# RWKV row pairs of a fused fp32 kernel: the 16x16 diagonal blocks of the chunk inverse move from TensorE products to elementwise VectorE work with transfers through DRAM, some row tensors move into PSUM banks, and the sums over 64 channels become two fp32r passes

## The reference, cut to what is touched

```python
k_mod = k.astype(f32) * (1.0 + (a - 1.0) * k_a)
kk = heads(k * k_k)
kk = kk / jnp.maximum(jnp.sqrt(jnp.sum(kk * kk, axis=-1, keepdims=True)), 1e-12)
def step(state, inp):
    r_t, w_t, k_t, v_t, aa_t, bb_t = inp
    sa = jnp.einsum('bhvk,bhk->bhv', state, aa_t)
    state = state * w_t[:, :, None, :] + sa[..., None] * bb_t[:, :, None, :] + v_t[..., None] * k_t[:, :, None, :]
    return state, jnp.einsum('bhvk,bhk->bhv', state, r_t)
...
var = jnp.mean(jnp.square(y - mean), axis=-1, keepdims=True)
y = ((y - mean) * lax.rsqrt(var + GN_EPS)).reshape(b, s, c) * lnx_w + lnx_b
bonus = (jnp.sum(r_h * k_h * r_k, axis=-1, keepdims=True) * v_h).reshape(b, s, c)
```

## Time and profile before

| | |
|---|---|
| runs, median of 3 | 2084.86 us (2081.75 to 2087.8) |
| profiled execution | 2081.08 us, of which the span is 2079.3 us |
| busy share of the span | PE 98%, PEld 81%, POOL 57%, DVE 55%, ACT 26% |
| mean granted TensorE clock | 0.995 |

### The profile page before, as it was taken

How to read it: one execution, slowest core, us unless ns; L and a number is a source line. 1 busy time by engine, 2 the same in 40 slices (tenths; PEclk the granted TensorE clock), 3 DMA queues, 4 the chain that set the end, 5 groups by cost and what they waited for, 6 DMA issues and landing times.

```text
span 2079.3 us, 39898 instructions
## 1 busy us (share of the span) xinstructions
PE 2031.4 (98%) x16195; PEld 1678.5 (81%) x16195; DVE 1139.5 (55%) x1533; ACT 536.0 (26%) x1139; POOL 1178.7 (57%) x1175
## 2 busy tenths in 40 slices
PE   8999999999999999999999999999999999999998
PEld 6888888877877787788877888888886888888886
DVE  6878624466667654202068677666773655555312
ACT  2100002233434212313143133333223023333101
...
GB/s 136 102 92 102 101 101 46 92 176 121 127 163 112 148 82 64 98 62 61 124 56 93 15 65 66 46 48 46 65 65 124 133 101 81 101 99 90 89 112 56
DMA packets 181243, 190.28 MB, mean 92 GB/s; under 512 B 8526, under 2 KB 162269, under 8 KB 180829
## 3 DMA queue, kind: packets, MB, share of 16 engines
q1 hardware_dynamic: 172288, 181.81, 27.6%
...
## 4 chain that ended last, share of the span: by engine, by line
PE 61%; DVE 3%; issue 1%; POOL 1%; DVEq 1%; POOLq 1%; ACT 0%; ACTq 0%
PE bank L915 8%; PE bank L916 8%; PE bank L917 8%; PE bank L1592 7%; PE bank L1553 3%; PE bank L1405 3%; PE bank L1421 2%; PE bank L1423 2%; PE bank L1422 2%; PE bank L1690 2%; PE bank L1327 1%; PE bank L1328 1%; PE bank L1329 1%; PE bank L1080 1%; PE bank L1294 1%
## 5 line engine op out<-in xcount | busy, mean ns | idle before, releaser
L740 POOL TENSOR_SCALAR whi<-raws 128x1024 fp32r<-128x1024 f32 (+5 forms) x312 | 321.0, 1029 | 284.9 <-PE bank L1082 166.8
L746 POOL TENSOR_TENSOR wlo<-raws,whi 128x512 fp32r<-128x512 f32 (+5 forms) x312 | 400.8, 1285 | 0.0
L745 POOL TENSOR_TENSOR wlo<-raws,whi 128x512 fp32r<-128x512 f32 (+5 forms) x312 | 373.4, 1197 | 46.0 <-issue 3.0
L915 PE MATMUL bank<-hbuf,whi 128*128 128x512 f32 (+2 forms) x840 | 329.4, 392 | 1.8 <-POOL wlo L746 1.8
L917 PE MATMUL bank<-hbuf,wlo 128*128 128x512 f32 (+2 forms) x840 | 327.8, 390 | 0.0
L916 PE MATMUL bank<-hbuf,whi 128*128 128x512 f32 (+2 forms) x776 | 303.0, 390 | 0.0
L649 POOL TENSOR_TENSOR spare<-ones 1x1 f32<-1x1 f32 x92 | 21.4, 233 | 298.5 <-PE bank L917 208.2
L915 PEld LDWEIGHTS bank<-hbuf,whi 128*128 128x128 f32 (+2 forms) x840 | 157.1, 187 | 37.0 <-POOL wlo L746 3.1
L917 PEld LDWEIGHTS bank<-hbuf,wlo 128*128 128x128 f32 (+2 forms) x840 | 157.1, 187 | 34.1
L916 PEld LDWEIGHTS bank<-hbuf,whi 128*128 128x128 f32 (+2 forms) x776 | 145.2, 187 | 31.1
L672 POOL TENSOR_SCALAR lg2L<-lg 128x128 fp32r<-128x128 f32 x8 | 2.4, 298 | 221.7 <-DMA lg<-in_g 221.7
...
## 6 DMA issues: line engine op xcount, KB each, us to landing
...
raws<-in_w_in SPq DMA_DIRECT2D x41, 512.0 KB, 3.9
...
```

The source lines that it names most:

```text
L740: G.tensor_scalar(h_, r_, 1.0, 1.0, ALU.mult, ALU.mult)
L745: G.tensor_tensor(first[0], first[1], f32(first[2]), ALU.subtract)
L746: G.tensor_tensor(last[0], last[1], f32(last[2]), ALU.subtract).then_inc(raw_split, 1)
L915: M.matmul(dst, wh, acts[k][0], start=(first and k == 0), stop=False)
```

## The change

It has four parts.

1. **Block inverse.** `LEVELS` keeps 5 products in 4 levels, those that join blocks of 16 to 32 and 64. The 16x16 blocks are inverted by VectorE on 64 partitions (`inverted_blocks`), one block per partition and pair of columns. For that `diagonal_blocks` packs the blocks out of the product D, ACT writes them to DRAM and reads them back with a block on a partition (`blocks_gathered`), and the result goes the same way back (`blocks_kept`, `blocks_spread`), a chunk later each, and is spread by VectorE (`spread_blocks`) into `V` and `W`. The product D now stands in `gates`, after 6 matmuls.
2. **Row in PSUM banks.** Squares, key directions, lengths, decays and deviations of a row use banks 3, 4, 5 and 7 in place of tiles of SBUF; the factor of the decays moves into ACT's scale; `finished` moves from the wide part into the next chain.
3. **Sums.** For rows 2 to 7 each head sum takes two fp32r matmuls: ACT makes the upper part by a cast, VectorE the lower part by a subtraction, and each sum waits for `sum.lo`.
4. **Slots.** The 12 products left in `prepare` stand in slots 1, 2, 6, 7, 9, 10, 12, 14, 16, 17, 19 and 21; slots 0, 3 to 5, 8, 11, 13, 15, 18, 20, 22 and 23 are empty.

The core of the diff:

```diff
-    (("DA", "D", "N2"), ("D", "DA", "A2")),
-    (("N2", "A2", "A4"), ("A2", "U", "U")),
-    (("A4", "U", "V"),),
-    (("A4", "V", "V"),),
-    (("A4", "V", "V"),),
-    (("V", "I", "W"), ("E16", "V", "Z")),
+    (("E16", "V", "Z"),),
     (("W", "Z", "V"), ("Z", "W", "W")),
     (("E32", "V", "Z"),),
     (("W", "Z", "last"),),
...
+BLOCKS_KEPT_AT = (3, 2, 2, 2, 2, 2, 3)
...
-LEVEL_BANK = ((1, 6),) * 7 + ((7,), (6,))
+LEVEL_BANK = ((1,), (1, 6), (7,), (6,))
+D_AFTER = 6
...
+            def head_sums(dst, q, which):
+
+                hi, lo = sum_split(q, which)
+                pe.wait_ge(sem("sum.lo"), sum_number(q, which))
+                M.matmul(dst[:, :], same64[:, :], hi, start=True, stop=False)
+                return M.matmul(dst[:, :], same64[:, :], lo, start=False, stop=True)
+
...
-                rkv(0, 2)
+                rkv(0, 6)
                 if q >= 2:
                     variances(q - 2)
-                rkv(2, 8)
+                rkv(6, 8)
                 if q >= 2:
                     pe.wait_ge(sem("inv.dve"), q * TAKEN_ALL)
-                    bonus_sums(q - 1)
                 else:
                     pe.wait_ge(sem("gt.taken"), 2)
-                rkv(8, 16)
+                rkv(8, 10)
+                if q >= 2:
...
 
                 pe.wait_ge(evac[0], fill("rkv", 0) + q + 1)
-                for n in range(3 * DT):
+                for n in range(D_AFTER):
                     gate_part(q, n)
-                pe.wait_ge(sem("rk.bonus"), q)
-                pe.wait_ge(sem("rk.y"), q)
+                gram(q, "D")
+                for n in range(D_AFTER, 3 * DT):
+                    gate_part(q, n)
+                pe.wait_ge(sem("rk.sig"), q + 1)
                 for n in range(3 * DT, 6 * DT):
                     gate_part(q, n)
 
...
+            def upper_sum(q, which, x):
+
+                A.copy(sum_split(q, which)[0], x).then_inc(sem("sum.hi"), 1)
...
+                    A.activation(tile(sq, 0), Kr[:, :], ACT.Square, scale=pcol[q % 3][:, 5:6]).then_inc(sem("rk.sq"), 1)
+                else:
+                    act.wait_ge(sem("gn.v"), q - 1)
+                    A.activation(bank[7][:, :], Kr[:, :], ACT.Square, scale=pcol[q % 3][:, 5:6])
+                    act.drain()
+                    upper_sum(q, "key", bank[7][:, :])
...
+            def blocks_gathered(q):
+
+                act.wait_ge(sem("blk.d"), q + 1)
+                act.dma_start(blocks_in[q % 2].rearrange("(c p j) -> p c j", c=CHUNKS, p=P),
+                              diagonal.rearrange("p (c j) -> p c j", c=CHUNKS)).then_inc(sem("blk.kept"), 16)
+                act.wait_ge(sem("blk.kept"), 16 * (q + 1))
+                act.dma_start(blk, blocks_in[q % 2].rearrange("(n x) -> n x", n=64)).then_inc(sem("blk.in"), 16)
+
+            def blocks_kept(q):
+
+                act.wait_ge(sem("blk.x"), q + 1)
+                act.dma_start(blocks_out[q % 2].rearrange("(w n x) -> n w x", w=2, n=64),
+                              hf[0:64, 0:2 * BLK * BLK].rearrange("n (w x) -> n w x", w=2)).then_inc(sem("blk.out"), 16)
+
+            def blocks_spread(q):
+
+                act.wait_ge(sem("blk.out"), 16 * (q + 1))
+                act.dma_start(hf[:, S + P:S + 3 * P].rearrange("p (x j) -> p x j", j=BLK),
+                              blocks_out[q % 2].rearrange("(x p j) -> p x j", p=P, j=BLK)).then_inc(sem("blk.back"), 16)
+
             def take_gates(q):
 
                 take_gate(q, 0)
+                if q >= 2:
+                    blocks_gathered(q)
                 take_gate(q, 1)
 
 
...
                     A.copy(sa[:, :], bank[5][:, cs]).then_inc(sem("sq.se"), 1)
+                    if p + 1 < PAIRS and c == BLOCKS_KEPT_AT[p]:
+                        blocks_kept(p + 1)
+                    if p + 1 < PAIRS and c == BLOCKS_KEPT_AT[p] + 1:
+                        blocks_spread(p + 1)
                     if c + 1 < CHUNKS:
...
+            def key_directions(q):
+
+                lengths = bank[3]
+                dve.wait_ge(sem("rk.nr"), q + 1)
...
+                dve.drain()
+                V.scalar_tensor_tensor(lengths[:, :], Kr[:, :], pcol[q % 3][:, 5:6], lengths[:, :], ALU.mult, ALU.mult)
...
+                V.scalar_tensor_tensor(aT[par][:, :], direction[:, :], -1.0, lwd[:, :], ALU.mult, ALU.mult)
+                dve.drain()
+                V.tensor_tensor(direction[:, :], direction[:, :], cc[:, :], ALU.mult)
+                dve.drain()
+                V.tensor_tensor(bT[:, :], direction[:, :], aa[:, :], ALU.mult).then_inc(sem("rk.ab"), 1)
+                dve.drain()
+                V.tensor_scalar(change[:, :], aa[:, :], pc[:, 6:7], pc[:, 10:11], ALU.mult, ALU.add)
...
+
+            def lower_sum(q, which, x):
+
+                hi, lo = sum_split(q, which)
+                dve.wait_ge(sem("sum.hi"), sum_number(q, which))
+                V.tensor_tensor(lo, x, f32(hi), ALU.subtract).then_inc(sem("sum.lo"), 1)
...
                     columns_of(q)
+                    lower_sum(q, "variance", gn_sq[:, :])
                     log_decays(q)
+                    lower_sum(q, "bonus", Rr[:, :])
                     take_key(q)
                 take_bonus(q - 1)
+                if 2 <= q < PAIRS:
+                    lower_sum(q, "key", bank[7][:, :])
                 if more:
                     take_product(q, 0, Rr)
-                if q >= 2:
+                if q == PAIRS:
+                    deviations(q - 2)
                     finished(q - 2)
-                if more:
+                if q == 1:
                     take_product(q, 2, vT[q % 2])
...
-                gram("D")
-                taken(inv_D, 1, "up16")
+                if q >= 2:
+                    inverted_blocks(q)
                 gram("A")
...
-                take_level(0)
-                take_turned(vtok, 7, "rk.tv")
                 if q == 0:
                     key_directions(1)
-                take_level(1)
+                if q < 2:
+                    inverted_blocks(q)
+                else:
+                    finished(q - 2)
                 gram("qb")
                 taken(Gqb[q % 2], 0, "up0")
-                take_level(2)
+                take_turned(vtok, 7, "rk.tv")
+                take_turned(kN, 0, "rk.tk")
                 take_turned(bN[q % 2], 7, "rk.tb")
-                take_level(3)
-                take_turned(kN, 0, "rk.tk")
-                take_level(4)
-                gram("qk")
-                taken(Gqk, 7, "up0")
                 if q == 0:
+                    gram("qk")
+                    taken(Gqk, 7, "up0")
                     decayed_keys(1)
...
+                dve.wait_ge(sem("blk.back"), 16 * (q + 1))
+                spread_blocks(V, inv_D, blk_v).then_inc(sem("inv.v"), 1)
+                spread_blocks(V, tile(hf, 0), blk_w).then_inc(sem("inv.w"), 1)
+                if q:
+                    gram("qk")
+                    taken(Gqk, 7, "up0")
+                else:
+                    dve.drain()
+                for k in range(len(LEVELS)):
                     take_level(k)
                 dve.drain()
+                if q == 0:
+                    diagonal_blocks(1)
+
+            def diagonal_blocks(q):
+
+                dve.wait_ge(sem("rk.block"), q + 1)
+                masked(inv_D, bank[1], "up16")
+                dve.drain()
+                V.tensor_reduce(diagonal.rearrange("p (c j) -> p c j", c=CHUNKS),
+                                inv_D[:, :].rearrange("p (c b j) -> p c j b", c=CHUNKS, j=BLK), AX.X, ALU.add)\
...
+            def inverted_blocks(q):
+
+                dve.wait_ge(sem("blk.in"), 16 * (q + 1))
+                V.memset(blk[:, 0:BLK * BLK:BLK + 1], 1.0)
...
+                for m in (4, 8):
+                    n, cube = BLK // (2 * m), [64, m, m, m]
+
...
+                    def times(lefts, rights):
+                        for b in range(n):
+                            terms = blk_terms[:, b * m ** 3:(b + 1) * m ** 3]
+                            V.tensor_tensor(terms.rearrange("n (i j k) -> n i j k", i=m, j=m),
+                                            lefts[b].unsqueeze(2).to_broadcast(cube),
+                                            rights[b].rearrange("n k j -> n j k").unsqueeze(1).to_broadcast(cube),
+                                            ALU.mult)
+                        dve.drain()
...
+                    half = blk_half[:, 0:n * m * m]
+                    V.tensor_reduce(half, blk_terms[:, 0:n * m ** 3].rearrange("n (x k) -> n x k", k=m), AX.X, ALU.add)
+                    dve.drain()
...
+                V.tensor_copy(blk_t.rearrange("n (j i) -> n j i", j=BLK), blk.rearrange("n (i j) -> n j i", j=BLK))\
+                    .then_inc(sem("blk.x"), 1)
...
                 if p + 2 < PAIRS:
                     key_directions(p + 2)
                     decayed_keys(p + 2)
+                    diagonal_blocks(p + 2)
+                    decayed_queries(p + 2)
```

(2 more changed lines are left out.)

312 lines of the change are left out of this document (192 added, 120 removed).

## The result

The changed kernel takes 2112.5 us (median of 4 runs, 2107.1 to 2119.3), the kernel before beside it 2086.1: a ratio of 1.0128 with a 95% interval of 1.0108 to 1.0149, some 27 us slower. The profiled executions are 2107.1 and 2081.1 us, 26.0 apart. The forecast of 2075 and its range are missed on the slow side, beyond every rival's time.

A forecast was written before the change was run, and what follows sets the result against it. It took TensorE, busy 98%, as the bound. Chains 0 to 5 -21.6, wide stretches +1.2, block waits +10.5, prologue and chain 6 zero: -9.9 us, 2071.2 profiled, 2075 as median; range 2048 to 2094.

The forecast's parts named there:

- every rival's time: Whole kernel: nothing waits 2057 (23%), late transfers 2096 (15%), TensorE clock falls 2087 (12%), slow block inverse 2090 (8%).
- The slots: Chains 0 to 5: eight emptied slots give 3.6 us inside a chain, slot 23 gives 1.15, together 4.75.
- Nearly no wait: Slot 6 of a chain: VectorE has the blocks inverted at S+6.0, and slot 6 begins at S+7.5.
- E32: Not a run: a result VectorE takes in the chain after the block inverse, forecast at S+7.3, before slot 6.
- The transfers back: Store 2.1 and read 3.3 us of inverted blocks; V at S+15.9, slot 14 waits 0.45 us.
- The wide stretch: From chain end T to next chain: bT at T+23.0, D waits 1.7, 33.4 us against 33.2.
- Prologue 0: Before the first chain: gains and round-trip waits sum to 0, bounds -4 and +5, with 0.5 us for half clock.
- Chain 6 gives nothing: Last chain but one, beside busy GpSimd: priced at no gain; the other bound was a gain of 4.75 us.
- my bound of 9: VectorE's 16x16 block inverse in a chain: priced at 6.3 us, bounded by 5 and 9.
- The clock: Rival, 12%: TensorE's clock halves in emptier chains, up to 1.7 us for each of seven, 2087.

The follow-up runs named there:

- e11: Changed kernel with all reorderings: e6, e7, e10, the deviations of e9, and the bonus sum two slices later; 2097.7 us, ratio 1.0057.
- e13: e12 without GpSimd's later start and with two more filled products before slot 9 of chain 6; 2091.3 us, ratio 1.0022.
- e6: Changed kernel with VectorE's prologue reordered: pair 0's returned blocks spread before the keys and queries of pair 1; 2104.4 us, ratio 1.0086.
- e1: Changed kernel with extra unread products put into TensorE's waits or emptied slots, in the prologue and chains 0 to 6; 2099.5 us, ratio 1.0060.
- e12: e11 with extra unread products in the remaining waits of the prologue and chains 0 and 6; 2098.6 us, ratio 1.0050.
- e7: Changed kernel with GpSimd starting the mixing stage's splits only after the last block inverse; 2105.0 us, ratio 1.0090.
- e9: e5 with the deviations of pair 6 in an SBUF tile in place of a PSUM bank; 2076.8 us, ratio 0.9956.
- e5: Changed kernel with the earlier products in place of the block inverse and its transfers, keeping PSUM banks and new sums; 2080.0 us, ratio 0.9971.
- e10: Changed kernel with three of VectorE's takes moved between the halves of the block inverse, pairs 2 to 7; 2103.3 us, ratio 1.0066.

## Why the prediction was wrong

- **The slots** were right. Behind an empty slot `sa` follows after 0.65 us, `state` after 0.76, `rhs` after 0.74, as taken:

```profile
1306.33 0.21 ACT L2338 COPY rhs<-bank 128x64 f32<-128x64 f32 x1 [0.85 <-PE bank L1728]
1306.98 0.21 ACT L2344 COPY sa<-bank 128x64 f32<-128x64 f32 x1 [0.43 <-PE bank L1728]
1307.74 0.32 ACT L2351 ACTIVATE state<-bank,fade 128x64 f32<-128x64 f32 x1 [0.55 <-PE bank L1769]
1308.48 0.21 ACT L2338 COPY rhs<-bank 128x64 f32<-128x64 f32 x1 [0.43 <-PE bank L1728]
1311.59 0.21 ACT L2344 COPY sa<-bank 128x64 f32<-128x64 f32 x1 [2.89 <-PE bank L1728]
```

- **"Nearly no wait" at slot 6** failed: 1.6 to 2.15 us in each of chains 1 to 5 (the last row above is its effect). In chain 2, S, the first of the chain's products, is 1301.06. TensorE reaches slot 6 at S+7.5, just as I had it; the mis-sized term is VectorE's series, which has E32 at S+9.1 and not at S+7.3. The gathered blocks landed at S+1.0 in place of S-0.9, since their read took 4.1 us and not about 2, so the block inverse starts at S+1.1 in place of S-0.3; and it takes 6.75 us and not 6.3, with large multiplications of 1.02 us where I had 0.69. Chain 2, with the clock at 1.00, is 1.8 us shorter where I had 2.75. The read is slow when SyncE's weight loads run beside it. Windows of the read for pair 3, and for pair 7, where no such load is issued:

```profile
1297.99:1302.00 4.01, 4.01 (x46) 3.20 (x46) 2.93 (x2) 0.59 (x1) 0.00 (x0) 1.00 0.92 271
1545.13:1547.20 2.07, 2.07 (x10) 1.70 (x10) 2.00 (x2) 0.00 (x0) 0.00 (x0) 1.00 0.13 32
```

  For pairs 2 to 6 two loads of 512 KB are issued 1.5 to 1.6 us before the read, and the transfer engines are busy 0.76 to 0.93 of it. In e11 to e13 the loads stand 4.7 to 5.3 us before it, and the same read takes 2.0 to 2.4 us (once, 2.4 us behind the loads, 3.1). For pair 3 in e13:

```profile
1292.38:1294.48 2.10, 2.10 (x47) 1.67 (x47) 0.75 (x1) 0.63 (x2) 0.00 (x0) 1.00 0.36 107
```

- **The transfers back** were priced right, 2.4 and about 3.1 us. V comes at S+17.5 against S+15.9 and TensorE is at slot 14 at about S+17.4 against S+15.5: both are shifted by the wait at slot 6. Slot 14 waits 0.57 us in chain 1, 0.52 in chain 4 and under 0.2 in chains 2, 3 and 5. Chain 0 waits 2.65 and 3.16 us at slots 9 and 14 (I had 2.5 and 3.3).
- **The wide stretch** was nearly right: `bT` at T+22.8 (23.0), the bonus sum waits 0.7 to 1.5 us (1), D 0.45 to 0.63 (1.7). It is 0.6 us longer than before where I had 0.2.
- **"Prologue 0"** failed: +7.0, 2 beyond its bound. The step had the round trips, but not that VectorE, in its written order, comes to the returned blocks 7.4 us late (e6: -5.0), and 0.5 us for the clock, which stands at 0.50 from 1148.5 to 1169.0, from behind a wait of 2.30 us on through that of 7.44 (e1: -4.3; both repaired, e12: -6.0).
- **"Chain 6 gives nothing"** failed, and is the largest term: +10.6 there, and 13.4 to the end of chain 7. I had read GpSimd's 27.75 busy us beside it as a bound on the gain only, and carried the block inverse at its quiet price into the one chain where GpSimd works, though two rows of mine had the factor (0.69 and 1.61 us). There the block inverse takes 11.42 us (e7: 6.8), above my bound of 9, the read back 5.8 in place of 3. The last chain's 4.0 us are the reciprocal that moved ahead of its start (e9 against e5: -2.3) and half clock (e1: -1.7).
- **The clock** was a rival at 12%, one stretch of 3.41 us per chain. The mechanism came about and its size was off: 61.4 us at 0.50 against 3.4. TensorE's busy time fell by 36 us and not by some 60, in part since products at 0.50 take longer. In the prologue and in chains 0 and 6 TensorE's waits on VectorE bring it, for there e1 filled the waits themselves. In chains 3 to 5 the cause is not shown: there e1 filled the emptied slots, so the thin chain and the wait of 1.6 to 2.15 us behind it were changed together, and chains 1 and 2, as thin and with waits of 1.95 and 1.73 us, stay at 1.00. The Trainium skill (TensorE: Matmul & The Clock Gate, Part 1) has only activity release the clock; e1, which adds idle-time work and gains 13 us, agrees.

Prologue 7.0, the 1.7 ahead of it, chain 0 0.9, chains 1 to 5 10.3, wide 2.7 and the end 13.4 are the 36 us between -9.9 and +26.0. Chain 0's share is uncertain by the 3.4 us that it differs between e10 and the changed kernel.

Shown by a run of their own: the half clock, VectorE's order in the prologue, GpSimd's part in chain 6, the last chain's reciprocal, the price of the sums. For VectorE's order, GpSimd's part and the reciprocal it is the windows that show it, since the intervals of the ratios overlap those of the kernels that were edited. Shown by rows of several runs, without an experiment made for it: that the gathered read is slow beside the loads. Only argued: that the slower read back in chain 6 comes of the loads beside it (its share of DMA is 0.35 against 0.15).
